# Two modulation chunks at the head of each dense FFN, and the residual scaled ahead of row copies

## The reference, cut to what matters

```python
def adaln(cond, w, b):
    d = w.shape[0]
    m = jax.nn.silu(cond) @ w + b
    return [m[:, None, i * d:(i + 1) * d] for i in range(6)]

def modulate(x, g, shift, scale):
    return rmsnorm(x, g) * (1.0 + scale) + shift

def swiglu(h, wg, wu, wd):
    return (jax.nn.silu(h @ wg) * (h @ wu)) @ wd
```

## Time and profile before

| | |
|---|---|
| median of 3 runs | 2861.36 us (2860.82 to 2863.77) |
| the profiled execution | 2857.08 us, span 2855.3 us |
| TensorE matmul busy | 2610.9 us, 91% of the span |
| VectorE busy | 1950.6 us, 68% |
| ScalarE busy | 1426.0 us, 50% |
| memory read | 671.79 MB, 236 GB/s over the span |

### The profile page before, as it was taken

One profiled execution on the slowest core, in us unless ns is written; L12 is line 12 of the kernel. 1 busy time (PEld: TensorE's weight loads), 2 busy tenths in 40 slices (PEclk: granted clock), 3 DMA queues, 4 the chain that ended last, 5 costly groups with the idle time before them and its releaser, 6 DMA issues. The chain is left out here.

```text
span 2855.3 us, 58215 instructions
## 1 busy us (share of the span) xinstructions
PE 2610.9 (91%) x23038; PEld 1971.6 (69%) x23038; DVE 1950.6 (68%) x2630; ACT 1426.0 (50%) x1733; POOL 14.9 (1%) x12
## 2 busy tenths in 40 slices
PE   6977899999887779989899989879999999999997
PEld 3744677676664457767667767658888888888885
DVE  3266455555545665555656555669999999999996
ACT  3146344343321544444344444357777677777764
POOL 0000000000200000000000000000000000000000
PEclk7989999999998889999899999889999999999999
DMA  6340455454466026536265546239999999999994
GB/s 267 118 192 1 168 213 208 164 203 163 170 261 251 15 103 232 203 140 232 96 245 200 198 160 228 91 132 393 388 400 379 381 389 380 390 382 375 395 377 163
DMA packets 121211, 674.36 MB, mean 236 GB/s; under 512 B 13488, under 2 KB 13968, under 8 KB 67088
## 3 DMA queue, kind: packets, MB, share of 16 engines
q1 hardware_dynamic: 119376, 661.88, 61.4%
q10 hardware_dynamic: 1728, 11.01, 1.0%
HBM read 671.79 MB, written 1.05 MB: 236 GB/s over the span
## 5 line engine op out<-in xcount | busy, mean ns | idle before, releaser
L889 PE MATMUL ps<-projected,normed_or_mix 128*128 128x256 bf16 x1504 | 409.9, 273 | 2.4 <-issue 2.4
L890 PE MATMUL ps<-projected,normed_or_mix 128*128 128x256 bf16 x1504 | 409.9, 273 | 0.0
L1109 PE MATMUL ps<-projected,turned 128*128 (+1 forms) x1792 | 303.1, 219 | 0.5 <-DVE turned L1221 0.5
L1109 PE MATMUL ps<-projected,normed_or_mix 128*128 (+1 forms) x1792 | 303.1, 219 | 0.2 <-DVE normed_or_mix L1221 0.2
L1110 PE MATMUL ps<-projected,turned 128*128 (+1 forms) x1792 | 303.1, 219 | 0.0
L1111 PE MATMUL ps<-projected,turned 128*128 (+1 forms) x1792 | 303.1, 219 | 0.0
L1110 PE MATMUL ps<-projected,normed_or_mix 128*128 (+1 forms) x1792 | 303.1, 219 | 0.0
L1111 PE MATMUL ps<-projected,normed_or_mix 128*128 (+1 forms) x1792 | 303.1, 219 | 0.0
L1226 DVE TENSOR_TENSOR aux<-weights,aux 128x1024 bf16<-128x1024 f32 x224 | 273.1, 1219 | 0.4 <-ACT aux L1183 0.2
L1221 DVE TENSOR_TENSOR normed_or_mix<-weights,normed_or_mix 128x2048 bf16<-128x2048 f32 x112 | 256.1, 2287 | 6.4 <-ACT normed_or_mix L1177 6.4
L1221 DVE TENSOR_TENSOR turned<-weights,turned 128x2048 bf16<-128x2048 f32 x112 | 256.2, 2287 | 3.5 <-ACT turned L1177 3.5
(11 more groups left out here) (380 smaller groups left out, 5956.2 us busy)
## 6 DMA issues: line engine op xcount, KB each, us to landing
weights<-moe SPq DMA_DIRECT2D x224, 1024.0 KB, 7.6
weights<-moe SPq DMA_DIRECT2D x224, 512.0 KB, 5.7
weights<-l_ffn SPq DMA_DIRECT2D x66, 1024.0 KB, 5.0
weights<-ada SPq DMA_DIRECT2D x64, 1024.0 KB, 5.4
weights<-l_ffn SPq DMA_DIRECT2D x66, 512.0 KB, 5.5
weights<-ada SPq DMA_DIRECT2D x64, 512.0 KB, 6.0
weights<-ffn SPq DMA_DIRECT2D x28, 1024.0 KB, 5.1
weights<-w_in SPq DMA_DIRECT2D x24, 948.0 KB, 4.7
```

The costliest lines, as they stand in the source:

```text
L889: pe.matmul(o, hi, h_hi(k), start=(k == 0), stop=False)
L890: pe.matmul(o, hi, h_lo(k), start=False, stop=False)
L1109: pe.matmul(o, hi[:, t], xh, start=(k == 0), stop=False)
```

## The change

It does three things. Eight chunks move: the passages ahead of the three dense FFNs of layers 0, 1 and 2 take one chunk in place of three, the passage ahead of layer 1's input projection one in place of three, and layer 1's first head norm 11 in place of 12, while the input passage of the first scan layer takes three in place of two. Each of the four dense FFNs takes two chunks at its own head, with copies of the chunk functions that were defined further down before. There the 14 zero products become 2. And in every passage but the first, ScalarE copies only the first chunk's row ahead of the scaling of the residual, and the second behind it. `plan` follows. The rest of the program is the same.

```diff
     planned("ada", 3, 16)
     planned("l0_ffn", F0 // PB)
+    planned("ada", 2, 19)
     planned("l0_ffn", F0 // PB)
-    planned("ada", 3, 19)
+    planned("ada", 1, 21)
     planned("l1_w_in", 2 * len(SPLIT["l1_w_in"]))
-    planned("ada", 12, 22)
+    planned("ada", 11, 22)
...
+    ada_bank = lambda i: PS[:, (7, 6, 7, 0, 7, 0)[i], :]
+
+    def ada_row(pe, i, at=None):
+        at = place.n if at is None else at
+        arrived(pe, at + i)
+        if i >= 4:
+            pe.wait_ge(S.ada_out.sem, S.ada_out.at(i - 1))
+        for turn_ in range(KD // strips):
+            for j in range(strips):
+                k = turn_ * strips + j
+                mm = pe.matmul(ada_bank(i)[32 * j:32 * (j + 1), 0:WC], CS[:, k, :],
+                               RING[:, (at + i) % SLOTS, k * WC:(k + 1) * WC],
+                               start=(turn_ == 0), stop=(turn_ == KD // strips - 1))
+        mm.then_inc(S.ada_rows.sem, 1)
+
+    def ada_turn(pe, i):
+        pe.wait_ge(S.ada_kept.sem, S.ada_kept.at(i + 1))
+        for m in range(per):
+            t = pe.matmul(ada_bank(i)[:, WC + 4 * m:WC + 4 * m + 3], adar[:, i % 2, m * PB:(m + 1) * PB], fold[:, 0:3],
+                          start=True, stop=True)
+        t.then_inc(S.ada_cols.sem, 1)
...
-                for i in range(early, min(early + 2, batch)):
-                    keep_rows(act, i)
-                    if begin:
-                        keep_cols(act, i)
+                for i in range(early, min(early + 2, batch)) if begin else ():
+                    ada_copies(act, i)
+                if batch and not begin:
+                    keep_rows(act, 0)
                 act.wait_ge(S.hop_b.sem, S.hop_b.at(1))
                 for b in range(0, nb, 2):
                     act.activation(XN[:, b, :], xs[b], ACT.Copy, scale=r[:, b:b + 1]).then_inc(S.ready.sem, 1)
+                if batch > 1 and not begin:
+                    keep_rows(act, 1)
...
-                                 ahead={batch - 1: lambda: turn_some(5)} if late else
+                                 ahead={batch - 1: lambda: turn_some(5)} if begin else {} if own else
                                  {0: lambda: turn_some(5), 1: lambda: turn_some(KD)})
...
             pe.sem_inc(S.down_done.sem, 2)
-            zero_products(pe, 14, 6)
+            for i in range(ada_n):
+                ada_row(pe, i, ada_at)
+            zero_products(pe, 2 if ada_n else 14, 5)
             pe.wait_ge(S.hop_d.sem, S.hop_d.at(2))
...
             up(0, 0)
+            for i in range(ada_n):
+                ada_turn(pe, i)
             with pe.Fori(0, rounds) as g:
...
             cast_hi(act, 0, 0, 0)
+            for i in range(ada_n):
+                ada_row_kept(act, i)
             cast_hi(act, 0, 1, 1)
             cast_hi(act, 1, 0, 0)
+            for i in range(ada_n):
+                ada_cols_kept(act, i, ada_at)
...
-            make_lo(dve, 0, 0, 0)
+            if ada_n:
+                dve.wait_ge(S.hi_gu.sem, S.hi_gu.at(1))
+                dve_step(dve, dve.tensor_tensor(gu[0][1], RING[:, place.n % SLOTS, 0:2 * D], gu[0][0], ALU.subtract))
+                dve.wait_ge(S.ada_kept.sem, S.ada_kept.at(ada_n))
+                dve.sem_inc(front_used.sem, 1)
+            else:
+                make_lo(dve, 0, 0, 0)
             make_lo(dve, 0, 1, 1)
             make_lo(dve, 1, 0, 0)
+            if ada_n:
+                ada_bias(dve, ada_n, ada_at)
...
-        a, n = place.n, f // PB
-        products, silus, gating = ffn_parts(x, f, o, gate=gate, first=first)
+        a, n, beside = place.n, f // PB, 2
+        place.n += beside
+        products, silus, gating = ffn_parts(x, f, o, gate=gate, first=first, ada_at=a, ada_n=beside)
...
-    modulate([(X, 0, 3, 0), (XC, 0, 3, 1)], col("n_ffn", 0, KD), batch=3,
+    modulate([(X, 0, 3, 0), (XC, 0, 3, 1)], col("n_ffn", 0, KD), batch=1,
```

More of the change, by code:

```diff
@@ L282, in build @@
     planned("l0_ffn", F0 // PB)
+    planned("ada", 2, 19)
     planned("l0_ffn", F0 // PB)
-    planned("ada", 3, 19)
+    planned("ada", 1, 21)
     planned("l1_w_in", 2 * len(SPLIT["l1_w_in"]))
-    planned("ada", 12, 22)
+    planned("ada", 11, 22)
     planned("l1_uq", 2)
     planned("l1_ukv", 3)
-    planned("ada", 7, 34)
+    planned("ada", 7, 33)
     planned("l1_w_out", 2 * len(SPLIT["l1_w_out"]))
-    planned("ada", 3, 41)
+    planned("ada", 3, 40)
     planned("l1_ffn", F0 // PB)
     for layer in range(2):
-        planned("ada", 2 + layer, 44 + 11 * layer)
+        planned("ada", 3, 43 + 12 * layer)
         planned(f"w_in{layer}", 2 * len(SPLIT["w_in"]))
@@ L453, in ada_copies, with ada_bias @@
         keep_cols(act, i)
-    def ada_bias(dve, n):
-        c = plan[place.n][1]
+    def ada_bias(dve, n, at=None):
+        c = plan[place.n if at is None else at][1]
         o = ada[:, c * per:(c + n) * per, :]
@@ L464, in ada_done, with ada_row_kept, ada_cols_kept @@
             s.done(n)
+    ada_bank = lambda i: PS[:, (7, 6, 7, 0, 7, 0)[i], :]
[17 more added lines that the diff above has]
+        t.then_inc(S.ada_cols.sem, 1)
+    def ada_row_kept(act, i):
+        act.wait_ge(S.ada_rows.sem, S.ada_rows.at(i + 1))
+        if i >= 2:
+            act.wait_ge(S.ada_cols.sem, S.ada_cols.at(i - 1))
+        release(act)
+        act.activation(adar[:, i % 2, :], ada_bank(i)[:, 0:WC], ACT.Copy).then_inc(S.ada_kept.sem, 1)
+    def ada_cols_kept(act, i, at=None):
+        c = plan[(place.n if at is None else at) + i][1]
+        act.wait_ge(S.ada_cols.sem, S.ada_cols.at(i + 1))
+        act.activation(ada[:, c * per:(c + 1) * per, :],
+                       ada_bank(i)[:, WC:WC + 4 * per].rearrange("p (m c) -> p m c", c=4)[:, :, 0:3],
+                       ACT.Copy).then_inc(S.ada_out.sem, 1)
     def feed_batch(block, n):
@@ L512, in modulate @@
         r, ss, u = (SM[:, a:a + nb] for a in (16, 24, 20))
-        late = begin or own
         with nc.Block() as block:
@@ L939, in ffn_done, with ffn_parts @@
             s.done(n)
-    def ffn_parts(x, f, o, gates=None, gate=GB, first=0):
+    def ffn_parts(x, f, o, gates=None, gate=GB, first=0, ada_at=None, ada_n=0):
         a, n = place.n, f // PB * (NE if gates is not None else 1)
@@ L1066, in _ @@
             def _(sp):
-                feed(sp, a + SLOTS, a + n + SLOTS)
+                feed(sp, a + SLOTS, a + beside + n + SLOTS)
             @block.tensor
@@ L1080, in ffn @@
         ffn_done(n)
+        for sg in (S.ada_rows, S.ada_kept, S.ada_cols, S.ada_out):
+            sg.done(beside)
         S.hop_d.done(2)
@@ L1628, in build @@
     p1 = P[:, :].rearrange("p (b n) -> p b n", b=4)
-    modulate([(X, 1, 0, 0), (XC, 1, 0, 1)], col("n_mix", KD, KD), rows=1, batch=3, own=True,
+    modulate([(X, 1, 0, 0), (XC, 1, 0, 1)], col("n_mix", KD, KD), rows=1, batch=1, own=True,
              loads=((AUX[:, :], d["na_bias"]), (EX[:, 4608:5120], d["na_mask"])))
@@ L1650, in build @@
               + [(nh(p1[:, b, NK:NK + 512], 64), nh(row(1, "qk")[:, 512:1024], 64), two(64, 512), None)
-                 for b in range(4)], batch=12)
+                 for b in range(4)], batch=11)
     turn(lambda b: p1[:, b, CQ:CQ + 384], 3, 2, lambda k: cqT[:, k, :], lambda k: col("qa", k))
@@ L1695, in build @@
     checkpoint(nc, "l1_mix", X)
-    modulate([(X, 1, 3, 0)], col("n_ffn", KD, KD), batch=3, gates=[(gate_row, 1, 5, 0)])
+    modulate([(X, 1, 3, 0)], col("n_ffn", KD, KD), batch=1, gates=[(gate_row, 1, 5, 0)])
     ffn(X, F0, 0)
@@ L2103, in build @@
         lay = 2 + layer
-        modulate([(X, lay, 0, 2)], col("n_mix", lay * KD, KD), rows=2 + layer, batch=2 + layer,
+        modulate([(X, lay, 0, 2)], col("n_mix", lay * KD, KD), rows=2 + layer, batch=3,
                  loads=((aw, d["gla_a_w"][layer]),))
@@ L2135, in build @@
         checkpoint(nc, f"s{layer}_mix", X)
-        modulate([(X, lay, 3, 2)], col("n_ffn", lay * KD, KD), batch=3 * (1 - layer),
+        modulate([(X, lay, 3, 2)], col("n_ffn", lay * KD, KD), batch=1 - layer,
                  gates=[(gate_row, lay, 5, 2)])
```

30 lines of the change are left out of this document (removed).

## The result

The changed kernel takes 2838.98 us, median of 4 runs (2837.12 to 2844.37), against 2861.61 us (2860.82 to 2863.77) for the kernel before on the same chip: ratio 0.9923, interval 0.9907 to 0.9939. That is 22.6 us less by the medians and 22.0 by the ratio; I had forecast 14.4 less, a time of 2847.0, and a range that ended at 2842. The profiled execution is the slowest of the four, 2844.37 us with a span of 2842.6. The sets of different experiments ran on different chips, so where two of them are compared the ratios to the kernel before are given too.

A forecast was written before the change was run, and what follows sets the result against it. The prediction took the short passages between stages, where one engine hands over to the next, as the bound. Its terms, -12.1 - 4.0 - 3.8 - 2.8 + 1.1 + 7.2 = -14.4 us, took 2861.36 to 2847.0 us, range 2842 to 2855.5.

The forecast's parts named there:

- three dense FFN passages: Passages ahead of three dense FFNs, three chunks become one: 4.0, 4.1 and 4.0 us less, together -12.1 us (-9 to -14).
- FFN heads: Two chunks at each of four dense FFN heads: late rows 0.4 and turns 1.4 us each, +7.2 us (+5.6 to +12).
- layer 1's projection passage: Ahead of layer 1's input projection, transfers decide and fewer bytes let it start sooner: -4.0 us (-3 to -5).
- head norm: Layer 1's head norm, 12 chunks become 11, one transfer less in a transfer-bound stretch: -3.8 us (-3.5 to -4.0).
- second scan stage: Second scan layer's input passage, scaling ahead of the second row copy: -2.8 us (-1.8 to -3.2).
- first scan stage: First scan layer's input passage, two chunks become three, with the new copy order: +1.1 us (0 to +2.5).
- I take 1.8 + 1.0: Second scan layer's input passage: 1.8 us for TensorE's wait ahead of the transposes, 1.0 for the third chunk's lost clock.
- The rule weighed: Shortened passages, mostly transposes: the skill says transposes don't engage full clock; the prediction went by a trace row where they did.
- 1, the heads eat the gain: FFN heads: clock falls under the first up products, four heads cost 20 us, total 2859.8 us; chance 0.08.
- 2, the ring: FFN heads: weight ring too shallow, item 2 lands late, four heads cost 30 us, total 2877 us; chance 0.04.
- 3, the transposes lose the clock: Five shortened passages: transposes run at low clock, some 8 us longer, total 2855 us; chance 0.05.
- 4, half the gain: Passages: another engine's chain or transfers hold each to half its gain, 8 us less, total 2855 us; chance 0.08.

## Why the prediction was wrong, point by point

Each term against the traces (before and after of the first comparison, unless said):

| term | forecast | measured | how |
|---|---|---|---|
| three dense FFN passages | -12.1 | -14.2 | scaling to cast: 15.86, 11.18, 11.77 to 11.11, 6.75, 6.75 |
| FFN heads | +7.2 | +5.8 | cast to next scaling (or cast): +1.36, +1.76, +1.35, +1.35 |
| layer 1's projection passage | -4.0 | -1.9 | scaling to next stage: 15.23 to 13.31 |
| head norm | -3.8 | about -3.2 | rest of that stage, means of all five traces with 12 chunks (335.2) and of the six with 11 and no edit there (332.0); single ones vary by 6 to 7; the chunks alone -3.8 at like clock, see below |
| second scan stage | -2.8 | -4.8 | means 182.66 and 177.90 |
| first scan stage | +1.1 | about -0.5 | means of three (178.7) and of two (178.2) |
| sum | -14.4 | -18.8 | |

Four terms were too small, by 7.1 us together, and two too large, by 2.7. That they take something off each other is luck.

**The step that failed first** is the price of the new order: "I take 1.8 + 1.0" for the second scan passage, and the same 2.8 taken off the third chunk of the first. The mechanism was right, the wait is gone and the third chunk runs at 1.50 us. The size was wrong, because I charged the lost clock to one row of the view, the 2.79 us of the third chunk, and stopped there; even that row alone gives back 1.29 and not the 1.0 that I took. The turns and transposes behind it are slow too, and the block behind the passage is about 1 us longer (169.6 against 168.5 us, means of two traces each). The passage itself lost 3.5 us (15.3 to 11.8), more than my upper bound of 3.2, and the stage 4.8. The order alone measured 5.9 to 8.6 us, and 8.0 to 9.4 on top of the moved chunks; my terms make 4.6 (2.8, and 1.8 for a passage of two chunks) and 5.6. The third chunk of the first scan passage then cost nothing in that passage: 11.4 us from first chunk to next stage before, 11.5 after (1256.48 to 1267.93), where I had 12.5. The run that keeps TensorE busy in the old wait shows that this is the clock: 5.4 us of the second scan stage came back, with the wait still there.

**The dense FFN passages**: mechanism and place as drawn (gates half slow, clock up behind them). I had the FFN 14.2 us behind the first chunk of the passage and it comes after 13.4. Half of the 0.8 us stands in the gates (they end 7.9 us behind the first chunk, I had 8.3) and half in the tail behind them (5.5, I had 5.9), the "estimate that keeps the durations of before". With the other two it makes 2.1 us too little in three passages, just beyond my bound of -14. One thing depends on the execution: layer 1's passage takes 6.75 us from scaling to cast in both traces of the changed kernel, and 7.9 in four of the eight traces with one chunk there, where its chunk ran at the low clock throughout (2.79 us).

**FFN heads**: in three of the four the passage ahead leaves the clock high, the chunks take 2.79 us and TensorE then waits 2.33, so the first product is 0.1 us later than before. Only in the second FFN of layer 0, with no passage ahead, they take 4.36 us at low clock, and the first product comes 0.5 us later. The mean is 0.2 where I took 0.4. The turns cost 1.26 where I took 1.4, and only because of their place: ahead of the wait three of four heads got them for nothing. My 0.9 us for the first four zero products doesn't follow from the 14 in 4.87, which make 1.4; the trace of the kernel before has the four in 1.02 us, and the forecast doesn't hang on it.

**Layer 1's projection passage**: that it is bound by transfers was right. That fewer bytes shorten the landing in proportion was wrong: with 2.1 MB less it went from 16.4 us to 14.4 only. The tables stood ahead on the same queue, and the order of issue decides (6.5 us when the parameters go first).

**Head norm**: the term was right for the chunks at like clock. From the first pair to the last chunk it is 40.5 and 40.6 us in the traces of the kernel before and 36.8 in the second trace of the changed kernel, 3.8 less. Where the stretch ran at the low clock it is 38.0 with 11 chunks (first trace of the changed kernel), and 41.5 and 42.1 with 12 (the order alone; the kernel before with early row parameters), again about 3.8 less. The first comparison sets a stretch at high clock before against one at low clock after, and so shows 2.5. What I missed is that the stretch has a second pace: "nothing else takes the place" was said of VectorE, and at the low clock TensorE's chain of products and turns takes 4.09 us a chunk and is the bound for a while. Which of the two an execution gets hides what a passage ahead gives back.

**The rule weighed.** In the dense FFN passages the transposes ran at the full clock, and my choice of the row held there. Ahead of layer 1's projection they began at the low clock, 32 in 6.06 us, and the granted clock rose under them, 0.50 up to 724 us, 0.78 to 726, then 1.00; the second trace has the same (6.12 us; 0.50, 0.68 and then 1.00 in its last three stretches of 2 us). That is what the earlier trace rows show too. The Trainium skill, "TensorE: Matmul & The Clock Gate", Part 4, says that transposes don't engage the full clock. By that rule the dense passages would have lost their clock and this one would have stayed at the low level; neither the 20 in 2.38 us behind the gates nor the rise under the 32 agrees with it. The slow start cost nothing here, as the copies were still done 2.8 us ahead of the row parameters.

**The rivals.** 1, the heads eat the gain: no, the clock is up when the first products start in all four heads; one head lost it in the run with early turns. 2, the ring: no; the FFNs are longer by what their heads show alone, so no round waits for weights. 3, the transposes lose the clock: no; in one passage they began without it, and the time was hidden. Its price also took 32 transposes for one passage alone, and the projection's has 32 too (x32 above). 4, half the gain: it was true of the projection passage alone.

**What stays open.** The terms sum to 18.8 us, the medians differ by 22.6 and 21.1. The profiled spans, 2855.3 and 2856.4 against 2842.6 and 2835.3, differ by 16.9. Stages that the change doesn't touch vary by some 3 us from trace to trace (289.89 to 293.63 for the first, 983.80 to 986.94 for the last), so I can't place the remaining 2 to 4. Why the same passage in the old order gives a stage of 182.60 and 182.72 us in the kernel before and of 185.39 with the moved chunks isn't settled either. The instructions are the same. The clock is much the same around the first transposes (0.82 and 0.77 granted in the 4 us that begin 0.8 us ahead of them), and differs in the next 4 us (0.75 against 0.50).

## What to carry to other kernels

When a wait of TensorE is costed, the clock behind it is part of its price, and it has to be followed past the end of the passage until the rows run at full clock again; in the second scan stage it was worth more than the wait. Small work was free in a wait in three heads of four and at full price behind it, so ask on which side of the wait each moved piece stands, and look at the clock behind it. And a place that is bound by transfers can be bound by the chain of small products for a while when the clock is low: compare traces at like clock before a transfer is priced.

## What was not expected of the hardware

- Behind an idle time of 1.80 us and 10 transposes the granted clock fell to 0.50, the level of 1.2 GHz, and stayed there for 12 us, in most of which TensorE ran short products and turns. With four zero products in that wait it was 1.00 behind it (181.29 and 180.01 us for the two stages in place of 185.46 and 185.39).
- Of three transfers issued within 1 us on one queue, 1280 KB landed 6.5 us after its issue as the first and 14.4 as the third. The 2048 KB beside it landed after 8.8 us as the first and after 13.6 as the second.
- The same program has two paces in the head norm, 3.77 us a chunk where transfers are the bound and 4.09 where the clock is low, and which of them it has for how many chunks changes from one execution to the next.
